# Hybrid decoder step: VectorE scales the prompt's attention probabilities, GpSimd leaves the loop

## The reference

```python
s = jnp.einsum('btgrd,bngd->bgrtn', q, kc[:, :, 0]) * ATTN_SCALE
s = jnp.where(mask, s.astype(jnp.float32), -jnp.inf)
m = jnp.max(s, axis=-1, keepdims=True)
e = jnp.where(mask, jnp.exp(s - m), 0.0)
return e / jnp.maximum(jnp.sum(e, axis=-1, keepdims=True), 1e-30)
...
return gates[..., 0, None] * o_cmp + gates[..., 1, None] * o_sel + gates[..., 2, None] * o_win
```

## Time and profile before

| | us |
|---|---|
| median of 3 runs | 3086.37 |
| lowest and highest | 3079.68, 3093.54 |
| the profiled execution | 3092.72 |
| its span in the trace | 3090.9 |
| busy in the span: PE / PEld / DVE / ACT / POOL | 2815.1 / 2599.9 / 1126.4 / 784.3 / 258.0 |
| mean granted clock of TensorE, share of full | 0.953 |

### The profile page before, as it was taken

One profiled execution on the slowest core, in us unless ns is written; L12 is line 12 of the kernel. 1 busy time (PEld: TensorE's weight loads), 2 busy tenths in 40 slices (PEclk: granted clock), 3 DMA queues, 4 the chain that ended last, 5 costly groups with the idle time before them and its releaser, 6 DMA issues.

```text
span 3090.9 us, 50695 instructions
## 1 busy us (share of the span) xinstructions
PE 2815.1 (91%) x21103; PEld 2599.9 (84%) x21103; DVE 1126.4 (36%) x1606; ACT 784.3 (25%) x1174; POOL 258.0 (8%) x243
## 2 busy tenths in 40 slices
PE   4999999996788687669999999999999999999998
PEld 3549999996666543449989999999999999999998
DVE  2322222226444553664433333233333333333333
ACT  1223111114344230142322122221222222122233
POOL 0000000000366101320100000000000000000002
PEclk9999999997799898679999999999999999999999
DMA  5135323322000554222222322223222222222222
GB/s 193 55 110 171 95 88 95 88 68 73 1 1 1 186 191 157 69 91 87 89 82 89 95 88 90 93 88 95 88 93 90 89 95 88 95 88 91 92 88 89
DMA packets 251880, 287.14 MB, mean 93 GB/s; under 512 B 21549, under 2 KB 244139, under 8 KB 247814
## 3 DMA queue, kind: packets, MB, share of 16 engines
q1 hardware_dynamic: 249214, 239.99, 25.0%
q0 software_dynamic: 2592, 46.14, 3.9%
HBM read 273.68 MB, written 20.71 MB: 95 GB/s over the span
## 4 chain that ended last, share of the span: by engine, by line
PE 80%; DVE 8%; POOL 4%; issue 2%; ACT 2%; DMA 2%; SPq 0%; ACTq 0%; POOLq 0%; DVEq 0%
PE PS L610 67%; POOL prob L1198 4%; PE PS L382 4%; DMA seg_raw<-in_cache_kv_cmp,idx_c 1%; PE PS L1100 1%; DVE c_tmp L1665 1%; DMA win_t<-kvs_tok 1%; PE PS L1370 1%; DVE seg_ord L464 1%; PE PS L368 1%; PE PS L1334 1%; DVE st_s L1901 1%; PE PS L1859 1%; PE PS L998 0%; PE PS L997 0%
## 5 line engine op out<-in xcount | busy, mean ns | idle before, releaser
L597 DVE TENSOR_TENSOR w_lo<-w_raw,w_hi 128x1024 fp32r<-128x1024 f32 (+1 forms) x388 | 460.3, 1190 | 1387.7 <-ACT w_hi L591 1386.7
L591 ACT ACTIVATE w_hi<-w_raw 128x1024 fp32r<-128x1024 f32 (+1 forms) x388 | 395.5, 1024 | 1501.1 <-PE PS L610 1501.1
L610 PE MATMUL PS<-h_hi,w_hi 128*128 128x260 f32 x3360 | 675.7, 283 | 7.4 <-DVE w_lo L597 5.1
L610 PE MATMUL PS<-h_lo,w_hi 128*128 128x260 f32 x3360 | 675.5, 283 | 0.0
L610 PE MATMUL PS<-h_hi,w_lo 128*128 128x260 f32 x3360 | 674.3, 282 | 0.0
L610 PEld LDWEIGHTS PS<-h_hi,w_hi 128*128 128x128 f32 x3360 | 516.6, 189 | 8.3 <-issue 7.5
L610 PEld LDWEIGHTS PS<-h_lo,w_hi 128*128 128x128 f32 x3360 | 519.3, 189 | 0.0
L610 PEld LDWEIGHTS PS<-h_hi,w_lo 128*128 128x128 f32 x3360 | 518.3, 189 | 0.0
L610 PE MATMUL PS<-u_hi,w_hi 128*128 128x260 f32 x2048 | 411.6, 282 | 8.4 <-DVE u_lo L2246 8.4
L610 PE MATMUL PS<-u_lo,w_hi 128*128 128x260 f32 x2048 | 410.8, 282 | 0.0
L610 PE MATMUL PS<-u_hi,w_lo 128*128 128x260 f32 x2048 | 410.3, 282 | 0.0
(11 more groups left out here) (384 smaller groups left out, 2580.7 us busy)
## 6 DMA issues: line engine op xcount, KB each, us to landing
w_raw<-in_w_up SPq DMA_DIRECT2D x256, 256.0 KB, 2.8
w_raw<-in_w_down SPq DMA_DIRECT2D x256, 256.0 KB, 2.9
w_raw<-in_w_in SPq DMA_DIRECT2D x160, 256.0 KB, 2.9
w_raw<-in_w_out SPq DMA_DIRECT2D x64, 256.0 KB, 3.1
out_kv_win_s<-in_state_kv_win SPq DMA_DIRECT2D x8, 1022.0 KB, 7.4
win_t<-in_state_kv_win SPq DMA_DIRECT2D x16, 448.0 KB
xtok<-in_x_prompt SPq DMA_DIRECT2D x4, 1024.0 KB, 9.2
x_r<-in_x_prompt SPq DMA_DIRECT2D x4, 1024.0 KB, 6.2
```

Source lines behind the costliest of these rows:

```text
L591: ins = e.activation(hi, raw, ACT.Copy)
L597: ins = e.tensor_tensor(lo, raw, hi.bitcast(F32), ALU.subtract)
L610: mm = e.matmul(PS[:, bank + 2 * m + h, 0:HN], w, x[:, k0 + k, h * HN:h * HN + HN], start=st and c == 0, stop=sp and c == 2)
```

## The change

`att_pool` is deleted with its call. Its four multiplications stand in `factors` on VectorE, directly behind the instruction that writes `fac`, with a wait for that instruction. Only the last of the four counts up `as_sc`, so TensorE's `turn` waits for u + 1 where it waited for 4 (u + 1). The wait in `factors` by which `fac` could not be overwritten while GpSimd read it is gone. The arithmetic is the same, element by element.

```diff
@@ att_pe
-                e.wait_ge(as_sc, 4 * (u + 1))
+                e.wait_ge(as_sc, u + 1)
@@ att_dve, factors
                 ch.step(e.reciprocal(rec[:, u % 2], den[:, u % 2]))
                 ch.settle()
-                if u >= 2:
-                    e.wait_ge(as_sc, 4 * (u - 1))
                 e.tensor_tensor(fac[:, u % 2], rec[:, u % 2], gv[:, h, 1 + b, :], ALU.mult).then_inc(as_fac, 1)
+                e.wait_ge(as_fac, u + 1)
+                for qt in range(4):
+                    p = prob[:, u % 2, P_OFF[qt]:P_OFF[qt] + (qt + 1) * P]
+                    last = e.tensor_scalar(p, p, fac[:, u % 2, qt:qt + 1], None, ALU.mult)
+                last.then_inc(as_sc, 1)
@@
-        def att_pool(e):
-            for u in range(NU):
-                e.wait_ge(as_fac, u + 1)
-                for qt in range(4):
-                    p = prob[:, u % 2, P_OFF[qt]:P_OFF[qt] + (qt + 1) * P]
-                    e.tensor_scalar(p, p, fac[:, u % 2, qt:qt + 1], None, ALU.mult).then_inc(as_sc, 1)
@@ the program of GpSimd
             values_pool(e)
-            att_pool(e)
             smp_pool(e, ch)
```

## The result

| | before | changed kernel |
|---|---|---|
| median, beside each other | 3084.3 (4 runs) | 3042.07 (4 runs) |
| median, in a second comparison | 3090.2 (9 runs) | 3036.03 (5 runs) |
| ratio, 95% interval | | 0.986 (0.9828 to 0.9892); 0.9834 (0.9809 to 0.986) |
| span of the profiled execution | 3090.9 | 3042.5 |
| first to last start of a transpose (line 1100) | 805.1 to 1021.3 = 216.2 | 801.7 to 970.7 = 169.0 |

The account below looks back on a forecast made before the run. A ring through GpSimd's multiplication, 6.91 us a turn, bounds the attention loop, with TensorE's 5.64 us as floor. Terms 3.0 + 1.3 + 36.4 + 2.2 = 42.9 us; 3086.4 - 42.9 = 3043.5 us, range 3034 to 3060.

Parts of the forecast that it names:

- the ring: Attention loop's cycle of transposes, VectorE's two copies, factor, GpSimd's multiplication, transposes again; period 6.91 us a turn.
- The pass: The four multiplications by the factor, moved to VectorE in each turn: 1.4 us, between 1.3 and 1.95.
- First turn: Start of the attention loop: transposes no longer wait for GpSimd's multiplication, only for TensorE's last scores; gain 3.0 us.
- From u = 0 to u = 1: Second turn of the loop: TensorE's clock may rise earlier; gain 1.3 us, between 0 and 2.65.
- The 29 intervals from u = 1 to u = 30: Steady turns of the loop: TensorE's idle time goes, 200.45 us become 164.0 us; gain 36.4 us.
- From u = 30 to u = 31: Last turn interval, without scores to fill the wait for copies: gain 2.2 us at full clock, 0.5 at half.
- The margins: Waits behind the moved multiplication in each turn: nothing is late, the tightest margins are 0.7 to 0.9 us.
- The gathers: GpSimd's sample-stage gathers start some 9 us ahead of the loop's end; nothing won, any cost under 1 us.
- A: Later row maxima in the loop push exponentials and copies past TensorE's need, taking part of the gain; 3057 us; chance 0.12.
- B: VectorE no faster at the multiplication than GpSimd's 4.26 us, so VectorE bounds the loop; 23 us slower, 3109 us; chance 0.04.
- C: Loop's gain partly lost in sample and state-space stages as TensorE's clock falls; half left is 3065 us; chance 0.06.
- D: TensorE's 5.64 us a turn holds gaps that close, or clock stays up; some 5 us more, 3038 us; chance 0.04.

Follow-up runs that it names:

- no_pass: Changed kernel with the multiplication of the probabilities by the factor left out; 3040.5 us, ratio 0.9842 to the kernel before.
- the two runs without the low part: Products of queries with the low part of the keys left out, in the changed kernel 3026.3 us and in the kernel before 3093.1 us.
- pass_twice: Changed kernel with the multiplication made twice on VectorE, the second time by a column of ones; 3053.1 us, ratio 0.9875 to the kernel before.
- rowmax_first: Changed kernel with the multiplication on VectorE placed behind the next turn's row maxima; 3042.3 us, ratio 0.9833 to the kernel before.
- pass_three_times: Changed kernel with the multiplication made three times on VectorE, twice by a column of ones; 3095.9 us, ratio 1.0024 to the kernel before.
- after_again: The changed kernel run once more without any edit; 3036.0 us, ratio 0.9834 to the kernel before.
- split: Changed kernel with GpSimd keeping the blocks of 128 and 256 columns, VectorE taking 384 and 512; 3036.7 us, ratio 0.9827 to the kernel before.
- before_no_low: Kernel before, without the products of the queries with the low part of the keys; 3093.1 us, ratio 1.0018 to the kernel before.

## Why the prediction was right, and the term that wasn't

**The bound and the new bound.** That GpSimd's pass was on the ring and TensorE's work would be the next floor was right; no_pass and the two runs without the low part show it from both sides.

**The pass** was put at 1.4 us between 1.3 and 1.95. It measured 1.27 us, with 285 to 485 ns for its four instructions, a little below the low end; the earlier trace rows were the right rows. The estimate by the formula of the Trainium skill, "VectorE: DVE Perf Modes", section on the TRN2 errata, was 0.91 us and too low. The size hardly mattered: no_pass shows that a shorter pass gives nothing. A longer one up to 1.95 us was not run; with the 3.33 us from pass_twice the ring would take 5.3 us, just under TensorE's 5.41, and only the first transposes would have come later.

**The sum**, term by term, with 0.3 us taken off, by which the changed kernel came earlier to the loop (last row of scores at 801.42 for 801.74):
1. First turn: 805.06 to 801.67, so 3.1 us; 3.0 forecast.
2. From u = 0 to u = 1: 807.75 - 801.67 = 6.08 us against 7.84, so 1.8 us; 1.3 forecast, between 0 and 2.65. The clock rose at about 804 us for 811, though not early enough for the upper end. The Trainium skill, "TensorE: Matmul & The Clock Gate", part 1, says that sustained activity releases the slow clock; the trace agrees, but the upper end that I had read from it did not come. Granted clock of 802 to 806 us, 0.77 in the mean:

```profile
802.00:806.00 4.00, 4.00 (x23) 3.70 (x22) 3.46 (x11) 2.52 (x9) 0.00 (x0) 0.77 0.00 0
```

3. The 29 intervals from u = 1 to u = 30: 965.25 - 807.75 = 157.5 us, so 43.0 us; 36.4 forecast. **This is the term that was mis-sized**, by 6.6 us. The step was "TensorE's own work between two transposes is 6.91 - 1.72 = 5.19 us" and its like of 6.09. They measured 4.97 and 5.86, 0.22 and 0.23 us less. I had taken the period less the idle time as the work. But a matmul's row runs on to the end of its result, while the next one may start before: line 1117 shows 1.06 us in both kernels, and in the changed one the transposes start 889.46 - 888.57 = 0.89 us behind its start. That is 0.17 us of it. The rest, 0.06 us, is in the transposes themselves, 1.25 us in place of 1.31; they no longer come after a pause. The waits of the weight loads in the kernel before, 815 to 1010 us, would have told:

```profile
PEld PS L1100 <- POOL prob L1198: 41.1, 28, 1.9
PE PS L1100 <- POOL prob L1198: 35.7, 28, 1.7
```

With 41.1 / 28 = 1.47 us a turn in place of 1.27 the floor comes out at 5.44 us, and 29 turns give 42.6 us.
4. From u = 30 to u = 31: 969.75 - 965.25 = 4.50 us against 6.91, so 2.4 us; 2.2 forecast. Only the second of the two pauses was left (1.01 us), the clock stayed at 1.00, and values took 2.39 us in place of 4.09:

```profile
967.52 2.39 PE L1112 MATMUL PS<-kv_tok 128*128 128x512 f32 x8 [1.01 <-issue]
...
969.75 1.25 PE L1100 MATMUL PS<-ident,prob 128*128 128x128 f32 x10
```

Sum: 50.2 us in the loop; 42.9 forecast. The profiled execution, forecast at 3049.8 us, took 3044.38. The first comparison of medians gave 42 us, which looks like a hit; the second gave 54. The loop's 50 us lie within both intervals (33 to 53 and 43 to 59 us), so part of the closeness of 3043.5 to 3042.07 was luck of the runs.

**The margins.** The schedule from T, the start of the transposes, held, each row a little earlier than I counted: pass over at T + 3.75 for T + 3.95, row_max over at T + 5.35 for T + 5.6, last row sum at T + 6.22 for T + 6.5. rowmax_first and pass_twice show how close the next bounds are: 1.3 or 1.7 us more on VectorE between factor and transposes, and TensorE waits.

**The gathers** cost and bring nothing, as said. **Rivals:** A and B did not come. pass_twice and pass_three_times confirm their formula, but A's point was set by the floor that I had too high: with 5.41 us in place of 5.64 it lies at a pass of 2.1 us, not 2.26, close to my upper bound of 1.95. C's loss isn't seen: behind the loop the first trace has 2 us more than the kernel before (2067.3 against 2065.1) and after_again 7 us less. Its premise "nothing there waits for a fixed time, so only the clock could do it" was wrong, since TensorE waits there for the window rows (last section). D came in the form "TensorE's 5.64 us a turn holds small gaps that close", which had a chance of 0.04 and deserved a larger one.

## What to carry to other kernels

When a pass on a slow engine closes a ring, ask what the other engines' own work per turn is: that, not the pass's length, is what moving it can give; here 4.3 us of GpSimd time were worth 1.5 us a turn. An engine in the chain with idle time is a candidate to take the work as long as its own ring, with what queues behind the new work, stays under the new bound. Take the floor of an engine from the distances of starts where it runs without a pause, not from the period less its idle time, since the last record before a pause shows a tail that a next instruction would overlap.

## What the runs showed of the hardware

**GpSimd beside VectorE.** In split, GpSimd's row of 128 columns runs at the same time as VectorE's pass over SBUF (groups of 815 to 960 us):

```profile
L1204 POOL TENSOR_SCALAR prob<-prob,fac 128x128 f32<-128x128 f32 x27 | 27.4, 1015 | 95.1 <-DVE fac L1167 95.1
L1204 POOL TENSOR_SCALAR prob<-prob,fac 128x256 f32<-128x256 f32 x26 | 23.9, 920 | 0.0
```

It takes 1015 ns. In the kernel before, where VectorE was reading PSUM for the row maxima at that moment, it took 603 in the mean. The row of 256 columns, which runs beside row_max in both, takes 920 and 922 ns. So GpSimd's first row took 0.41 us more beside the 0.93 us pass. VectorE lost too: its row of 512 columns took 595 ns in the mean, against 481 in the changed kernel, where GpSimd is idle. "GPSIMD Engine Reference" of the Trainium skill, in its key points, has the engines share SBUF interfaces and names VectorE's two-port modes as a cause of contention; the numbers agree with it, though no run here changed the mode alone.

**Where runs of one program differ.** The first trace of the changed kernel and after_again have the same loop, but their spans differ by 10 us. Up to 1090 us they are within 1 us; then the sample stage's products with V (line 1365) take 4 us of it, 54.1 us from first to last start against 50.1, both at a granted clock of 0.97. In the first trace (the kernel before has such a wait too, 3.1 us):

```profile
1133.94 5.30 PE L1365 MATMUL PS<-sel_t,pT_s 128*16 128x256 f32 x16 [3.80 <-DMA win_t<-kvs_tok]
```

After_again has no such wait for the window rows, and its last product starts 4.9 us earlier. The other 5 us lie behind it, where the next stage runs at different clocks (first line the first trace, second line after_again):

```profile
1148.60:1204.60 56.00, 38.85 (x137) 22.89 (x138) 32.44 (x56) 3.79 (x8) 12.86 (x8) 0.63 0.17 57
```

```profile
1144.00:1200.00 56.00, 38.81 (x154) 23.51 (x154) 34.77 (x61) 6.29 (x13) 13.89 (x9) 0.73 0.17 57
```

With the same 38.8 us of TensorE's time after_again gets 154 matmuls done in place of 137. What decides whether the window rows are late, and whether the clock there follows from it, was not tried.

**Less work, lower clock.** In before_no_low TensorE has 22% of idle time in the loop against 18%, and its granted clock there is 0.94 against 1.00. Its loop is 1.4 us longer than with the work left in, and three turns hold nearly all of that: 7.01, 7.28 and 7.78 us in place of 6.91. They start at 893.70, 907.62 and 921.83 us, where the granted clock was low, 0.83 from 890 to 897 us, 0.80 from 904 to 911 and 0.78 from 918 to 925. An engine that waits anyway gained nothing by doing less, and in this one trace it paid a little in clock.
